# Convolution's normed tile turned back through VectorE's blocks and a main memory scratch, with its first turn one unit later

## The reference, cut to what matters

```python
def conv_module(xd, conv_w, conv_b, norm_g, norm_b):
    a, g = xd[..., :CONV_DIM], xd[..., CONV_DIM:]          # CONV_DIM = 256
    h = a * jax.nn.sigmoid(g)
    h = lax.conv_general_dilated(h, conv_w[:, None, :], window_strides=(1,),
        padding=[(CONV_WIDTH - 1, 0)], feature_group_count=CONV_DIM, ...) + conv_b
    return jax.nn.silu(layer_norm(h, norm_g, norm_b))      # the norm is over the 256 channels

merged = (gates[:, :, 0] * (ya @ w_proj_a[l]) + gates[:, :, 1] * (yb @ w_proj_b[l])
          + gates[:, :, 2] * (yc @ w_proj_c[l]) + gates[:, :, 3] * (yd @ w_proj_d[l]))
```

## Time and profile before

| | |
|---|---|
| median of 3 runs | 792.05 us (791.87 to 792.35) |
| the profiled execution | 791.93 us |
| its span, first to last instruction | 790.2 us, the remaining 1.7 us lie around it |
| busy PE / DVE / ACT / POOL | 782.9 / 620.5 / 431.2 / 141.3 us |
| mean granted TensorE clock | 0.998 |
| DMA | 155.39 MB, mean 197 GB/s |

### The profile page before, as it was taken

The page is one execution under the profiler, slowest core; times in us unless marked ns, Lnnn a source line. Parts: engine busy times, 40 slices in busy tenths (PEclk is TensorE's granted clock), DMA queues, the critical chain, the costliest instruction groups (busy, mean ns, idle before and its releaser), DMA issues.

```text
span 790.2 us, 15749 instructions
## 1 busy us (share of the span) xinstructions
PE 782.9 (99%) x6519; PEld 761.3 (96%) x6519; DVE 620.5 (79%) x769; ACT 431.2 (55%) x552; POOL 141.3 (18%) x148
## 2 busy tenths in 40 slices
PE   9999999999999999999999999999999999999997
PEld 8999999999999999999999999999999999999996
DVE  6899999876886766675698899998678767676764
ACT  6666887534654353434465569855365453434444
POOL 2315753083000000000000363513300000000000
PEclk9999999999999999999999999999999999999999
DMA  9975475666645566646568556575546465656541
GB/s 301 305 236 178 128 233 197 224 201 207 213 161 187 202 199 212 211 161 213 165 198 276 161 164 190 152 257 193 194 161 214 160 213 188 221 192 197 189 158 53
DMA packets 124332, 155.39 MB, mean 197 GB/s; under 512 B 5952, under 2 KB 107922, under 8 KB 124272
## 3 DMA queue, kind: packets, MB, share of 16 engines
q1 hardware_dynamic: 122736, 152.46, 59.4%
q0 software_dynamic: 1360, 1.82, 0.8%
q10 hardware_dynamic: 176, 0.27, 0.1%
HBM read 148.23 MB, written 1.05 MB: 189 GB/s over the span
## 4 chain that ended last, share of the span: by engine, by line
PE 94%; DVE 4%; ACT 1%; issue 1%; DVEq 0%; POOL 0%; ACTq 0%; POOLq 0%
PE bank L990 26%; PE bank L991 26%; PE bank L992 26%; PE bank L1080 3%; PE bank L1078 3%; PE bank L1081 3%; DVE w_lo L1406 2%; ACT w_hi L669 1%; PE bank L1050 1%; PE bank L1051 1%; PE bank L1052 1%; PE bank L1191 1%; PE bank L1038 0%; PE bank L1037 0%; PE bank L1039 0%
## 5 line engine op out<-in xcount | busy, mean ns | idle before, releaser
L990 PE MATMUL bank<-act,w_hi 128*128 128x256 f32 x1472 | 408.9, 278 | 0.8 <-DVE w_lo L1764 0.7
L991 PE MATMUL bank<-act,w_hi 128*128 128x256 f32 x1472 | 406.6, 276 | 0.0
L992 PE MATMUL bank<-act,w_lo 128*128 128x256 f32 x1472 | 406.6, 276 | 0.0
L1406 DVE TENSOR_TENSOR w_lo<-raw,w_hi 128x2048 fp32r<-128x2048 f32 x135 | 314.2, 2329 | 101.7 <-ACT w_hi L669 100.6
L669 ACT ACTIVATE w_hi<-raw 128x2048 fp32r<-128x2048 f32 (+3 forms) x146 | 265.2, 1825 | 128.1 <-PE bank L992 85.4
L990 PEld LDWEIGHTS bank<-act,w_hi 128*128 128x128 f32 x1472 | 276.3, 188 | 3.3 <-issue 2.4
L991 PEld LDWEIGHTS bank<-act,w_hi 128*128 128x128 f32 x1472 | 276.3, 188 | 0.5
L992 PEld LDWEIGHTS bank<-act,w_lo 128*128 128x128 f32 x1472 | 276.3, 188 | 0.0
L990 PE MATMUL bank<-y_hi,w_hi 128*128 128x256 f32 x288 | 79.7, 277 | 0.0
L992 PE MATMUL bank<-y_hi,w_lo 128*128 128x256 f32 x288 | 79.5, 276 | 0.0
L991 PE MATMUL bank<-y_lo,w_hi 128*128 128x256 f32 x288 | 79.5, 276 | 0.0
(11 more groups left out here) (251 smaller groups left out, 987.3 us busy)
## 6 DMA issues: line engine op xcount, KB each, us to landing
raw<-in_w_ffn_in SPq DMA_DIRECT2D x44, 1024.0 KB, 5.0
raw<-in_w_gate SPq DMA_DIRECT2D x32, 1024.0 KB, 5.3
raw<-in_w_ffn_out SPq DMA_DIRECT2D x22, 1024.0 KB, 4.9
raw<-in_w_in SPq DMA_DIRECT2D x18, 1024.0 KB, 5.8
raw<-in_w_o SPq DMA_DIRECT2D x8, 1024.0 KB, 5.0
raw<-in_w_proj_b SPq DMA_DIRECT2D x4, 1024.0 KB, 6.0
raw<-in_w_in SPq DMA_DIRECT2D x12, 256.0 KB, 5.4
gates<-qk SPq DMA_DIRECT2D x32, 64.0 KB, 5.5
```

The source lines that it names most:

```text
L990: nc.tensor.matmul(o, whi, ahi, start=first, stop=False, skip_group_check=skip)
L991: nc.tensor.matmul(o, whi, alo, start=False, stop=False, skip_group_check=skip)
L992: return nc.tensor.matmul(o, wlo, ahi, start=False, stop=last, skip_group_check=skip)
L1406: V.tensor_tensor(lo, raw[slot][:, :], hi.bitcast(F32), ALU.subtract).then_inc(lo_ready[slot], 1)
```

## The change

The tile is turned to tokens behind unit 22 and no longer behind unit 21. The norm moves from VectorE's step 21 to the head of its step 22, ahead of everything else in that step. TensorE's turn back to features, behind unit 22, goes away. In its place VectorE writes the normed tile in another column order (`conv_q`), turns its 32x32 blocks (128x512), SP writes the result to a scratch in main memory, waits, and reads it back by 4 DMAs of 64 KB so that blocks land in the right partitions (`conv_t`). ScalarE's gain, bias and tanh move from its step 22 to its step 23 and read `conv_t`. VectorE's multiplication moves from step 23 to the head of step 24. The low part for unit 27 stays in step 25.

```diff
 (SP)
+            def move_conv(l):
+                sp.wait_ge(conv_turned_ready, l + 1)
+                sp.dma_start(conv_blocks[l], conv_turned).then_inc(conv_out, 16)
+                sp.wait_ge(conv_out, 16 * (l + 1))
+                for q in range(4):
+                    sp.dma_start(conv_t[32 * q:32 * q + 32, :].rearrange("k (a y) -> k a y", a=4),
+                                 conv_blocks[l].rearrange("(a k) (q y) -> q k a y", a=4, q=4)[q]).then_inc(conv_in, 16)
...
+                    if u == 27:
+                        move_conv(l)
 (ScalarE)
-                if u == 22:
-                    act.wait_ge(ct2_done, l + 1)
+                if u == 23:
+                    act.wait_ge(conv_in, 64 * (l + 1))
                     for f in range(2):
...
+                    act.wait_ge(yd_scaled, 2 * (l + 1))
                     nc.scalar.activation(swish_t[:, :, :], yd_f[:, :, :], ACT.Tanh).then_inc(swish_ready, 1)
 (TensorE)
-                if u == 21:
+                if u == 22:
                     turn_conv(l)
-                if u == 22:
-                    bank_wait(l, 5, "cT2")
-                    pe.wait_ge(bank_free[5], free_at(l, 5, "cT1", True))
-                    for t in range(TT):
-                        for f in range(2):
-                            last = nc.tensor.transpose(bank[5][...], conv_n[:, t, f * P:(f + 1) * P], ident[:, :])
-                    last.then_inc(ct2_done, 1)
 (VectorE)
             def misc(l, u):
+                if u == 22:
+                    dve.wait_ge(ct1_done, l + 1)
...             (statistics and inverse root as they were in step 21)
+                    for t in range(TT):
+                        last = V.tensor_scalar(conv_q.rearrange("p (q f t x) -> p t f q x", q=4, f=2, t=TT)[:, t, :, :, :],
+                                               nat[:, t, :].rearrange("p (f q x) -> p f q x", f=2, q=4),
+                                               mv[:, t, 0:1], st[:, 10 + t:11 + t], ALU.subtract, ALU.mult)
+                    last.then_inc(bank_free[5], 1)
+                    dve.wait_ge(bank_free[5], free_at(l, 5, "cT1", True))
+                    dve.wait_ge(pt_in[2], 16 * PT_DMAS * (l + 1))
+                    V.transpose(conv_turned, conv_q).then_inc(conv_turned_ready, 1)
+                if u == 24:
+                    dve.wait_ge(swish_ready, l + 1)
+                    V.scalar_tensor_tensor(yd_f[:, :, :], swish_t[:, :, :], 1.0, yd_f[:, :, :], ALU.add, ALU.mult)
```

More of the change, by code:

```diff
@@ L131 @@
 BANKS[4] = ["S0", "S1", "S2", "S3", "PV2", "C", "D", "stat2"]
-BANKS[5] = ["S0", "S1", "S2", "S3", "cT1", "cT2", "C", "D"]
+BANKS[5] = ["S0", "S1", "S2", "S3", "cT1", "C", "D"]
 BANKS[6] = ["R1", "par", "wsT", "PV3", "C", "D"]
@@ L223, in build @@
         conv_n = part(sq[:, :, :], 12 * P, [TT, 256])
+        conv_q = part(sq[:, :, :], 12 * P, [4 * P])
+        conv_t = part(sq[:, :, :], 0, [4 * P])
+        conv_turned = turned[0][:, 0:4 * P]
+        conv_blocks = [nc.dram_tensor(f"conv_blocks{l}", [P, 4 * P], F32).ap() for l in range(L)]
         E = PAD + S
@@ L319, in build @@
         ct1_done = sem("ct1_done")
-        ct2_done = sem("ct2_done")
+        conv_turned_ready = sem("conv_turned_ready")
+        conv_out = sem("conv_out")
+        conv_in = sem("conv_in")
+        yd_scaled = sem("yd_scaled")
         yd_ready = sem("yd_ready")
@@ L821, in misc @@
                     last.then_inc(probs_ready, 1)
-                if u == 22:
-                    act.wait_ge(ct2_done, l + 1)
+                if u == 23:
+                    act.wait_ge(conv_in, 64 * (l + 1))
                     for f in range(2):
[L825 to L828, removed]
+                        nc.scalar.activation(yd_f[:, f, :].rearrange("p (t a x) -> p t a x", t=TT, a=4),
+                                             conv_t.rearrange("p (a f t x) -> p f t a x", a=4, f=2, t=TT)[:, f, :, :, :],
+                                             ACT.Identity, scale=half_cn[:, f:f + 1], bias=half_cn[:, 2 + f:3 + f])\
+                            .then_inc(yd_scaled, 1)
+                    act.wait_ge(yd_scaled, 2 * (l + 1))
                     nc.scalar.activation(swish_t[:, :, :], yd_f[:, :, :], ACT.Tanh).then_inc(swish_ready, 1)
@@ L1202, in misc @@
                     last.then_inc(pool_done, 1)
-                if u == 21:
+                if u == 22:
                     turn_conv(l)
-                if u == 22:
-                    bank_wait(l, 5, "cT2")
-                    pe.wait_ge(bank_free[5], free_at(l, 5, "cT1", True))
-                    for t in range(TT):
-                        for f in range(2):
-                            last = nc.tensor.transpose(bank[5][:, f * S + t * P:f * S + (t + 1) * P],
-                                                       conv_n[:, t, f * P:(f + 1) * P], ident[:, :])
-                    last.then_inc(ct2_done, 1)
             def ffn_in(l, u, use, b, nth):
@@ L1490, in misc @@
             def misc(l, u):
+                if u == 22:
+                    dve.wait_ge(ct1_done, l + 1)
+                    nat = bank[5][:, :].rearrange("p (t c) -> p t c", t=TT)
+                    for t in range(TT):
+                        link(l, V.bn_stats(bn6[:, t, :], nat[:, t, :]))
+                        V.memset(st[:, 14:15], 0.0)
+                        link(l, V.bn_aggr(mv[:, t, :], bn6[:, t, :]))
+                    link(l, V.tensor_scalar(st[:, 8:10], mv[:, :, 1], EPS, None, ALU.add))
+                    rsqrt(l, st[:, 10:12], st[:, 8:10], st[:, 12:14], ist[:, 2:4])
+                    for t in range(TT):
+                        last = V.tensor_scalar(conv_q.rearrange("p (q f t x) -> p t f q x", q=4, f=2, t=TT)[:, t, :, :, :],
[7 more added lines that the diff above has]
+                    dve.wait_ge(swish_ready, l + 1)
+                    V.scalar_tensor_tensor(yd_f[:, :, :], swish_t[:, :, :], 1.0, yd_f[:, :, :], ALU.add, ALU.mult)\
+                        .then_inc(yd_ready, 1)
+                if u == 25:
+                    lo_of(y_lo[:, 8:10, :], yd_f[:, :, :], y_hi[:, 8:10, :], 7, l).then_inc(ylo_ready, 1)
                 if u - 2 in ATT:
@@ L1493, in misc @@
                     dve.wait_ge(probs_ready, l * HP + hp + 1)
+                    if l and hp == 0:
+                        dve.wait_ge(conv_out, 16 * l)
                     if l or hp > 1:
@@ L1581, in misc @@
                     dve.sem_inc(params_free, 1)
[L1582 to L1602, removed]
                 if u in TAPS:
```

## The result

The changed kernel takes 795.35 us (median of 6 runs, 795.31 to 795.39) where the kernel before takes 791.87 (6 runs, 791.45 to 792.35). The ratio is 1.0043, with a 95% interval of 1.0033 to 1.0053: slower, by 3.5 us. The forecast was 796.0 in a range of 794.6 to 799.5. The profiled execution took 795.34, its span is 793.6 against 790.2.

A forecast was written before the change was run, and what follows sets the result against it. TensorE, busy for 782.9 of 790.2 us, was taken as the bound. Per layer −0.44 + 2.11 + 0.30 = +1.97 us, +3.9 for both, gave 796.0 us, with 794.6 to 799.5 as the range for 8 in 10.

The forecast's parts named there:

- one step: VectorE's step 22: norm and block turn ahead of gate_in(22), which frees bank 2, start that gate 5.14 us later.
- What leaves TensorE: Behind units 21 and 22: one of two groups of four transposes goes, saving 0.44 us per layer (0.44 to 0.59).
- Bank 2: At unit 23: TensorE waits for gate_in(22) to free bank 2, a stall of 2.11 us per layer (1.9 to 3.4).
- my allowances: Around VectorE's step 22: 0.1 us assumed per wake-up and 0.05 us for the block turn's wait on the bank.
- Bank 4: At unit 24: VectorE's subtraction that frees bank 4 slips, a second stall of 0.30 us per layer.
- Sum: Over each layer: −0.44 + 2.11 + 0.30 = +1.97 us, +3.9 us for both layers.
- The signs: In TensorE's new waits: about 2.1 us and 0.3, twice each; new waits should sum to the added time plus 0.9.
- The round trip: Scratch store and four loads: the tanh is ready at 159.3 with 1.5 us of slack before VectorE's step 24; costs nothing.
- The rival that it is late: Scratch round trip overruns its slack and delays unit 27: 797.8 us at 3.4 each way, 806 at 5.5; chance 0.22.
- The clock: TensorE in the stall: clock stays at 1.00; a rival has it slow, 1.4 to 2.8 us per layer, about 800; chance 0.03.
- The price by the page: VectorE's block turn: by the skill page's figure 1.24 us for four squares, making the sum 0.5 us per layer higher.

The follow-up runs named there:

- e5: The changed kernel with unit 23 taking bank 2 first (banks 2, 3, 0, 1 instead of 3, 0, 1, 2): 807.23 us.
- e4: The changed kernel with two more 256 KB copies within main memory between the scratch store and the four loads, each waited for: 803.9 us.
- e2: The changed kernel with first turn and norm back at unit 21, the scratch trip kept: 790.76 us, ratio 0.9981 to the kernel before.
- e8: The kernel before with TensorE's second group of transposes left out and nothing in its place: 791.06 us, ratio 0.9989.

## Why the prediction was right

The direction, the place and the size came from one step, and the runs bear it out.
- *What leaves TensorE:* 0.44 per layer forecast, 0.48 measured in the start of unit 23 (145.58 against 146.06). The two kernels that drop the other group of four, behind unit 22, gain 0.41.
- *Bank 2:* 2.11 forecast; 151.66 − (150.26 − 0.48) = 1.88 measured. The norm took 4.4 us as forecast, and its strided writes nothing more (0.99 against 1.00), the block turn 0.71 for 0.70, the gate 0.65 for 0.69. The difference is in my allowances: wake-ups of 0.02 to 0.06 and not 0.1, and a gate that starts 0.07 before the block turn's end, so that it ends 0.6 behind it and not 0.69.
- *Bank 4:* 0.30 forecast. Unit 24 starts 153.42 − 151.66 = 1.76 behind bank 2's first matmul, not 1.36. Of the 0.40, 0.24 is the wait (the step from 153.06 to 153.42 less the usual 0.12); the other 0.16 is that the first matmuls after a stop follow one another at 0.22 and 0.12 and not at 0.11. The prediction left that out. It comes once more at unit 24, 0.1.
- *Sum:* +1.97 per layer forecast, −0.48 + 1.88 + 0.40 + 0.10 = +1.90 measured, 3.8 for both. That the sum came so close is partly luck: bank 2 was 0.23 too dear, and the slow restarts, 0.16 and 0.10, were left out. The median moved by 3.48, because the kernel before carries 0.36 that the changed one lacks. I had taken the rest of the schedule as unchanged, which the rows of layer 1 seemed to support, and the chain of waits in the feed-forward stretch of layer 0 has VectorE in the lead and 0.41 us of unexplained issue time ahead of line 1698. It could have warned that something there may move; that the change would remove it, no row told. The rest of the 0.65 between forecast and result is the start of the sum: the kernel before was taken at 792.05 and its median over 6 runs is 791.87.
- *The signs:* the list of waits was to show 2.1 for bank 2 and 0.3 for bank 4, and the sum of new waits was to be the added time plus 0.9. The list shows 1.7 and nothing, 3.4 in all, because of what it leaves out. By the starts of the matmuls the sum is 2.38 per layer, 4.8 for both, against 3.8 added and 1.0 that left TensorE.
- *The round trip:* called free with 1.5 us of slack; it is free with 2.3. The four loads' issue, 0.44 each and not 0.59, and the landing, 2.0 and not 2.2, make the difference. The rival that it is late, 0.22, was worth its chance: with 6 us more it decides, and at the end of the chain 0.27 us were left where I had counted none.
- *The clock:* granted 1.00 in the stall, as forecast from 2.2 us of idleness at the span's end. Behind longer gaps it fell, with the price that e5 shows. The Trainium skill ("TensorE: Matmul & The Clock Gate", section "Why this matters for your kernels") warns of idle gaps between bursts of matmuls, after which the clock is back at half. The traces of e5 and of e4's layer 0 agree, with gaps of 5.9 and 3.4 us.
- *The price by the page:* the Trainium skill ("VectorE: DVE Perf Modes", section "The three transpose paths") has 311 ns for a bf16 square, which had given an estimate of 1.24 us for the block turn. The trace has 0.71, and the measurement decides.

## What to carry to other kernels

Where one engine is always busy, what counts of a moved step is which release stands behind it in an in-order queue. Here a 5 us step that was free beside unit 22 was put ahead of the instruction that frees bank 2, and 4.1 us of cover could not hold it; the same work behind that instruction left the layer as long as before, and at its old place it lets four transposes leave TensorE for a round trip through main memory at no price. Before reordering, find the next reader of each bank and buffer and count the matmuls that cover it. And compare differences of a few tenths of a microsecond with care: one instruction more that did nothing useful was worth 0.4 us.

## What the runs showed of the hardware

- A 256 KB store to main memory took 2.0 us alone and 5.1 beside two loads of 1 MB; a 256 KB copy within main memory 2.9; 64 KB back in 512-byte runs 2.0.
- Four fp32 transposes of 128x128 cost TensorE 0.41 us behind unit 22 (e2, e8) and 0.48 behind unit 21 (the changed kernel).
- After a stop the first matmuls started 0.22 and 0.12 us apart and not 0.11, so a stop of 1.88 us cost 0.16 more.
- A wait of 3.43 us was followed by a half clock, one of 3.11 in the same run was not. In e5 the half clock lasted some 4 us of steady work and cost about 2 us per layer.
- VectorE paused for 0.47 us at one instruction, and one unrelated instruction more in its program removed the pause.
